# The delta rule's inverse on four corners of the TensorE array, with the column decay made by TensorE

## The reference, cut to what matters

```
L[i, j] = beta_i * exp(g_i - g_j) * (k_i . k_j)     for j before i, 0 elsewhere
T       = (I + L)^-1
w, u    = T @ (beta * exp(g) * k),  T @ (beta * v)
```

## Time and profile before

| | us |
|---|---|
| median of 3 runs | 2218.81 |
| lowest, highest | 2217.07, 2221.3 |
| the profiled execution, its own time | 2219.51 |
| its span | 2217.7 |
| mean granted TensorE clock | 0.972 |
| TensorE busy, of the span | 2094.4 (94%) |
| VectorE busy | 1413.8 (64%) |
| ScalarE busy | 598.6 (27%) |
| GpSimd busy | 1160.8 (52%) |

### The profile page before, as it was taken

How to read it: one execution, slowest core, us unless ns; L and a number is a source line. 1 busy time by engine, 2 the same in 40 slices (tenths; PEclk the granted TensorE clock), 3 DMA queues, 4 the chain that set the end, 5 groups by cost and what they waited for, 6 DMA issues and landing times.

```text
span 2217.7 us, 33444 instructions
## 1 busy us (share of the span) xinstructions
PE 2094.4 (94%) x13922; PEld 1732.4 (78%) x13922; DVE 1413.8 (64%) x1808; ACT 598.6 (27%) x1239; POOL 1160.8 (52%) x664
## 2 busy tenths in 40 slices
PE   6989999999999999999999989989889888999998
PEld 4877788888777767787887668878888767888886
DVE  6366778478665546779578697878666655611622
ACT  2153220122235452220121232356424222200200
POOL 4633667666655444766665333633300555656654
PEclk9999999999999999999999999999999899999999
DMA  5321334334422112334435421112100112323321
GB/s 181 95 68 57 95 114 166 112 100 158 146 75 67 58 30 76 110 105 152 134 95 185 145 95 58 57 42 93 39 4 4 59 49 74 97 94 100 101 86 67
DMA packets 55767, 201.94 MB, mean 91 GB/s; under 512 B 6560, under 2 KB 6816, under 8 KB 54720
## 3 DMA queue, kind: packets, MB, share of 16 engines
q1 hardware_dynamic: 52272, 187.23, 26.1%
q0 software_dynamic: 1840, 9.60, 1.2%
q10 hardware_dynamic: 1504, 2.95, 0.5%
HBM read 194.78 MB, written 4.19 MB: 90 GB/s over the span
## 4 chain that ended last, share of the span: by engine, by line
PE 84%; DVE 9%; ACT 3%; issue 2%; POOL 1%; DMA 0%; SPq 0%; DVEq 0%; POOLq 0%; ACTq 0%
PE bank L536 69%; PE bank L2867 1%; PE bank L3131 1%; PE bank L2863 1%; POOL parts_r L517 1%; PE bank L2852 1%; PE bank L1448 1%; PE bank L1435 1%; PE bank L1940 1%; PE bank L1952 1%; PE bank L1752 1%; PE bank L1425 1%; DVE big L2284 1%; DVE big L2117 0%; POOL parts_r L511 0%
## 5 line engine op out<-in xcount | busy, mean ns | idle before, releaser
L536 PE MATMUL bank<-xn_r,parts_r 128*128 128x512 f32 (+1 forms) x2928 | 916.9, 392 | 37.8 <-DVE mix_r L776 13.5
L536 PE MATMUL bank<-big_r,parts_r 128*128 128x512 f32 x3208 | 925.4, 392 | 2.3 <-POOL parts_r L517 2.3
L517 POOL TENSOR_TENSOR parts_r<-ring,parts_r 128x1024 fp32r<-128x1024 f32 x293 | 738.6, 2521 | 24.4
L511 POOL TENSOR_SCALAR parts_r<-ring 128x1024 fp32r<-128x1024 f32 x293 | 343.9, 1174 | 724.0 <-PE bank L536 711.4
L536 PEld LDWEIGHTS bank<-big_r,parts_r 128*128 128x128 f32 x3208 | 601.9, 189 | 133.8 <-issue 5.1
L536 PEld LDWEIGHTS bank<-xn_r,parts_r 128*128 128x128 f32 x2928 | 554.0, 191 | 163.6 <-issue 39.0
L903 ACT ACTIVATE big<-bank,small 128x512 f32<-128x512 f32 x88 | 68.4, 780 | 409.1 <-DVE big L947 252.0
L932 DVE TENSOR_TENSOR bank<-bank,nb 128x512 f32<-128x512 f32 x88 | 61.3, 699 | 140.6 <-PE bank L536 140.6
L3398 DVE SCALAR_TENSOR_TENSOR h<-bank,vecs,h 128x512 f32<-128x512 f32 x24 | 17.9, 750 | 173.2 <-PE bank L536 173.2
L3472 DVE TENSOR_TENSOR big<-big 128x512 f32<-128x512 f32 x32 | 82.7, 2586 | 71.0 <-ACT big_r L3453 71.0
L547 DVE TENSOR_TENSOR big_r<-big,big_r 128x512 fp32r<-128x512 f32 x76 | 105.7, 1393 | 0.4
(11 more groups left out here) (460 smaller groups left out, 2767.6 us busy)
## 6 DMA issues: line engine op xcount, KB each, us to landing
ring<-weights SPq DMA_DIRECT2D x295, 512.0 KB, 3.6
cst<-mod_w SPq DMA_DIRECT2D x48, 512.0 KB, 3.9
h<-x SPq DMA_DIRECT2D x8, 256.0 KB, 7.7
h_store<-h POOLq DMA_DIRECT2D x8, 256.0 KB, 2.3
big<-consts POOLq DMA_DIRECT2D x2, 1024.0 KB, 8.9
h<-h_store POOLq DMA_DIRECT2D x1, 2048.0 KB, 8.9
out<-mix SPq DMA_DIRECT2D x8, 256.0 KB, 2.2
cst<-consts SPq DMA_DIRECT2D x1, 1300.0 KB, 11.8
```

What stands on the lines that cost most here:

```text
L511: pool.tensor_scalar(rounded(unit_parts(u)[0]), ring[:, u % RING], 1.0, 0.0, ALU.mult, ALU.add)\
L517: pool.tensor_tensor(rounded(lo), ring[:, u % RING], value(hi), ALU.subtract).then_inc(part_ready, 1)
L536: mm = pe.matmul(ps, rounded(w[a]), rounded(x[b]), start=(start and n == 0), stop=(stop and n == 2))
```

## The change

The inverse's matrix `X` of a cell now lies in the other half of the partitions than its `TT`.

- `gram` and `decay_rows` write to the other half (`across`), so `L`, `A` and `X` lie there. `product_x` takes both operands from that half and writes to the cell's own: the corners (64, 0) and (0, 64) in turn.
- Level 0 sets `X = I - A`. `turn_T` makes two things of it in one loop: its transpose (bank `3 + j`, which ScalarE copies to `Tm`, in the other half) and a copy moved to the cell's own half (bank `j`, which VectorE copies to `TT`). `STEPS` counts one step of TT more than `LEVELS`.
- `product_y` issues y and yt of one cell behind each other. y goes from the cell's own half to the other, yt from own to own; with the two halves in turn this uses all four corners.
- The column's -g_j is added by TensorE: `decay_rows` gets 16 more products, each of a 64x64 slice of g with a selector of -1, accumulated onto the same bank. They are also made for the four decays of `attend`. `decay_act` becomes one exponential over 512 columns in place of eight over 64.
- On VectorE the three loops over the units (L, then A, then TT with the mask of level 1) become one loop of four operations for each unit, followed by a loop that copies TT out of the bank; in the second group that copy waits for `right_u`. On TensorE and ScalarE the turn of a unit comes in its own round, and not one round later.

The level masks, the subtractions, the right sides and `attend` are otherwise as before.

```
-        sell[AG["decay"] + r, r] = sell[AG["beta"] + r, r] = 1
+        sell[AG["decay"] + r, r, 0:CH] = sell[AG["beta"] + r, r, 0:CH] = 1
+        sell[AG["decay"] + r, r, CH:] = -1
...
+        across = rows2[::-1]
+        cells = [(cols(bb, hd), r, x) for bb in range(2) for hd in range(GH) for r, x in zip(rows2, across)]
...
-        def decay_rows(pe, b_, d, pair, sel_, done, reader):
+        def decay_rows(pe, b_, d, pair, sel_, done, reader, place):
             for hd in range(GH):
-                for c, r in enumerate(rows2):
-                    mm = pe.matmul(ps[r, hd::GH], sel_[64:P, GH * d + hd, 0:CH], g_[:, 2 * pair[0] + c:2 * pair[1] + c + 1:2],
-                                   start=True, stop=True)
+                for c, r in enumerate(place):
+                    pe.matmul(ps[r, hd::GH], sel_[64:P, GH * d + hd, 0:CH], g_[:, 2 * pair[0] + c:2 * pair[1] + c + 1:2],
+                              start=True, stop=False)
+                for bb, b in enumerate(pair):
+                    for c, r in enumerate(place):
+                        mm = pe.matmul(ps[r, GH * bb + hd], g_[:, 2 * b + c], selL[64:P, GH * d + hd, CH:2 * CH],
+                                       start=False, stop=(bb == 1))
...
             def turn_T(u):
-                ps = grab(pe, SETS + j, dl(f"c{j}"), LEVELS * q + 1)
-                for c, r in cells:
-                    mm = pe.matmul(ps[r, c], TT[r, c], eye_c[r, :], start=True, stop=True)
+                turned = grab(pe, SETS + j, dl(f"c{j}"), LEVELS * q + 1)
+                moved = grab(pe, j, dl(f"TT{j}"), STEPS * q + 2)
+                for c, r, x in cells:
+                    pe.matmul(turned[x, c], X[x, c], eye_c[x, :], start=True, stop=True)
+                    mm = pe.matmul(moved[r, c], eye_c[x, :], X[x, c], start=True, stop=True)
...
             def product_x(u, n):
-                    mm = pe.matmul(ps[r, c], A[r, c], Tm[r, c], start=True, stop=True)
+                    mm = pe.matmul(ps[r, c], A[x, c], Tm[x, c], start=True, stop=True)
...
             def product_y(u, n):
-                    for c, r in cells:
-                        mm = pe.matmul(ps[r, c], TT[r, c], X[r, c], start=True, stop=True)
-                    mm.then_inc(dl(f"y{j}"), 1)
-                ps = grab(pe, j, dl(f"TT{j}"), LEVELS * q + n + 1)
-                for c, r in cells:
-                    mm = pe.matmul(ps[r, c], X[r, c], TT[r, c], start=True, stop=True)
+                yt = grab(pe, j, dl(f"TT{j}"), STEPS * q + n + 2)
+                for i, (c, r, x) in enumerate(cells):
+                    if n < LEVELS - 1:
+                        mm = pe.matmul(y[x, c], TT[r, c], X[r, c], start=True, stop=True)
+                        if i == len(cells) - 1:
+                            mm.then_inc(dl(f"y{j}"), 1)
+                    mm = pe.matmul(yt[r, c], X[r, c], TT[r, c], start=True, stop=True)
...
         def decay_act(act, ready, i, dst, done):
-            for bb, b in enumerate(pair):
-                for hd in range(GH):
-                    ins = act.activation(dst[:, cols(bb, hd)], dst[:, cols(bb, hd)], ACT.Exp,
-                                         bias=gd_sc[:, 0, b, GH * d + hd:GH * d + hd + 1])
+            act.activation(dst, dst, ACT.Exp).then_inc(dl(done), 1)
...
         def inverse_dve(dve):
                         dve.tensor_tensor(L, bank[j][:, :], X, ALU.mult).then_inc(dl("LT"), 1)
-                    for u in three:
                         dve.wait_ge(dl("LT"), u + 1)
                         dve.tensor_tensor(v8(A), v8(L), wide(level(d, 0)), ALU.mult).then_inc(dl(f"A{j}"), 1)
+                        dve.wait_ge(dl(f"A{j}"), LEVELS * q + 1)
+                        dve.tensor_tensor(v8(X), wide(eye_c), v8(A), ALU.subtract).then_inc(dl(f"TT{j}"), 1)
+                        mask_level(u, 1)
                 for u in three:
-                        dve.wait_ge(dl(f"A{j}"), LEVELS * q + 1)
                         if q:
                             dve.wait_ge(dl("ups"), 2 * (u - SETS) + 2)
-                        dve.tensor_tensor(v8(TT), wide(eye_c), v8(A), ALU.subtract).then_inc(dl(f"TT{j}"), 1)
-                        mask_level(u, 1)
+                        dve.tensor_copy(work[j][4], bank[j][:, :]).then_inc(dl(f"TT{j}"), 1)
```

More of the change, by code:

```diff
@@ L2823, in gram @@
                     for hd in range(GH):
-                        for r in rows2:
+                        for r, x in zip(rows2, across):
                             k_ = gd_k[0:GDN_D, hd, tokens(b, r)]
-                            mm = pe.matmul(ps[r, cols(bb, hd)], k_, k_, start=True, stop=True)
+                            mm = pe.matmul(ps[x, cols(bb, hd)], k_, k_, start=True, stop=True)
                 mm.then_inc(dl("gram"), 1)
@@ L2909, in attend @@
                     mm.then_inc(dl("qk"), 1)
-                decay_rows(pe, 7, d, pair, selA, "at_g", (dl("at_E"), i + 1))
+                decay_rows(pe, 7, d, pair, selA, "at_g", (dl("at_E"), i + 1), rows2)
             for q in range(GROUPS + 1):
@@ L2921, in inverse_pe @@
                         right_w(u - SETS)
-                    if q < GROUPS and u % SETS:
-                        turn_T(u - 1)
+                    if q < GROUPS:
+                        turn_T(u)
                     if q:
                         right_u(u - SETS)
-                if q < GROUPS:
-                    turn_T(SETS * q + SETS - 1)
                 if q == GROUPS:
@@ L2936, in inverse_pe, with decay_act @@
                         attend(n - 1)
-        def decay_act(act, ready, i, d, pair, dst, done):
+        def decay_act(act, ready, i, dst, done):
             act.wait_ge(dl(ready), i + 1)
-            for bb, b in enumerate(pair):
-                for hd in range(GH):
-                    ins = act.activation(dst[:, cols(bb, hd)], dst[:, cols(bb, hd)], ACT.Exp,
-                                         bias=gd_sc[:, 0, b, GH * d + hd:GH * d + hd + 1])
-            ins.then_inc(dl(done), 1)
+            act.activation(dst, dst, ACT.Exp).then_inc(dl(done), 1)
         def inverse_act(act):
@@ L2973, in inverse_act @@
                     for u in three:
-                        d, pair, j, _ = unit_of(u)
-                        decay_act(act, "E", u, d, pair, work[j][2], "D")
+                        decay_act(act, "E", u, work[u % SETS][2], "D")
                 for u in three:
@@ L2978, in inverse_act @@
                         take_w(u - SETS)
-                    if q < GROUPS and u % SETS:
-                        copy(u - 1, 0)
+                    if q < GROUPS:
+                        copy(u, 0)
                     if 0 < q < GROUPS:
                         take_u(u - SETS)
-                if q < GROUPS:
-                    copy(SETS * q + SETS - 1, 0)
                 if q == GROUPS:
@@ L2990, in inverse_act @@
                     if q == 0 and n <= TB:
-                        p, d = divmod(n - 1, 2)
-                        decay_act(act, "at_E", n - 1, d, (CB + 2 * p, CB + 2 * p + 1), at_decay[d], "at_D")
+                        decay_act(act, "at_E", n - 1, at_decay[(n - 1) % 2], "at_D")
         def inverse_dve(dve):
@@ L3080, in inverse_dve @@
                     if q < GROUPS:
-                        d, pair, j, _ = unit_of(u)
-                        L, A, X, Tm, TT = work[j]
-                        dve.wait_ge(dl(f"A{j}"), LEVELS * q + 1)
+                        j = u % SETS
+                        dve.wait_ge(dl(f"x{j}"), LEVELS * q + 1)
                         if q:
                             dve.wait_ge(dl("ups"), 2 * (u - SETS) + 2)
-                        dve.tensor_tensor(v8(TT), wide(eye_c), v8(A), ALU.subtract).then_inc(dl(f"TT{j}"), 1)
-                        mask_level(u, 1)
+                        dve.tensor_copy(work[j][4], bank[j][:, :]).then_inc(dl(f"TT{j}"), 1)
                 if q == GROUPS:
```

19 lines of the change are left out of this document (8 added, 11 removed).

## The result

The changed kernel takes 2227.49 us (median of 20 runs, 2218.13 to 2233.03) against 2221.11 for the kernel before (20 runs on the same chip, 2214.31 to 2228.78). The ratio is 1.0026, 95% interval [1.0016, 1.0036]: slower by about a quarter of a per cent, where 2204 was predicted.

What follows compares the result with a forecast made beforehand. TensorE sets 84% of the span; in the inverse's stage TensorE, VectorE or ScalarE bounds by part. +4.9 - 12.8 - 0.3 - 7.8 (group two's levels) + 1.5 = -14.5 us: 2205.0 profiled, 2204 median, range 2198 to 2222.

Steps and rivals of the forecast that it cites:

- The rate of a corner: `product_y` on four corners: a record each 14.6 ns, a unit's 64 records in 0.93 us where it took 1.87.
- rival B: Four corners give less: 23 ns a record whatever its columns, TensorE's level 7.2 us, 2213 us in all; chance 15%.
- C: y and yt of a cell leave two corners at work; `product_y` keeps 1.87 us, +8, 2227 us; chance 12%.
- D: A cell's second product can't start its weights before the first is done: 2.8 us a unit, 2249 us; chance 3%.
- First prologue: Start of the inverse's stage to group one's level 1: decays partly at half clock, then VectorE's path, +4.9 us on 16.35.
- Group one: First three units' five levels: 54.7 us become 41.9, -12.8 us.
- the halved `product_y`: Group one, four levels: 11.2 us of the gain.
- four decays: Group one: `attend`'s decay products on TensorE take back 3.7 us.
- ScalarE's block: Group one: the 2.02 us block of exponentials gone from between the levels, 5.3 us of the gain.
- Second prologue: Before group two's levels, 23.1 us: longer decays, last turn no longer waits, level 1 at +22.8, -0.3 us.
- The new copy: VectorE's copy of a whole bank of TT: between 0.47 and 0.69 us, taken as 0.61.
- Clock: Low granted clock stretches stay and one may be added through TensorE's gaps: +1.5 us, between 0 and 4.

Runs made afterwards that it cites:

- the pairs: Changed kernel, level products made for two cells at a time, half as many products, part of the result wrong: 2205.48 us against 2219.91 before.
- ScalarE's new order: Kernel before, attention's `decay_act` moved behind the next level's copies: 2216.06 us, ratio 0.9966; the same on four corners with exponentials back on ScalarE: 2212.35 us, 0.9958.
- the decay alone: Kernel before with only the column decay moved to TensorE, in wide products, one exponential a decay, two corners: 2226.40 us, ratio 1.0026.
- four corners without the decay: Changed kernel with the column decay back on ScalarE as eight exponentials, constant bias, result wrong: 2217.27 us, ratio 0.9983.
- idle corners filled: Kernel before with an added 64x64-weight, 4-column product on an idle corner for each `product_x` product in group two: 2235.72 us against 2222.41 before.
- the alternating weights: Kernel before with an added 32-weight-column, 4-streamed-column product ahead of each `product_x` product in group two: 2346.14 us.

## Why the prediction was wrong, step by step

**The rate of a corner: right, and not enough.** 14.6 ns a record is what the timeline shows inside `product_y`, between the stops. The step that failed is the next one, that a unit's 64 records then take 0.93 us and "TensorE's level falls from 8.40 to 5.6 us, so VectorE becomes the bound". The evidence for the rate were two bursts of 16 records, 32 instructions each with their weight loads; both fit many times into a block of 256. The argument against rival B, that the columns set the pace, was about the array, and nothing in the prediction asked what feeds it. A level is 288 records, 576 instructions: 576/256 x 3.6 to 4.0 is 8.1 to 9.0 us; the kernel before had 8.4. So group two stayed (41.4 in place of 31.9), and the pairs, which need half as many, gave 31.4.

By the 25 ns floor of the Trainium skill ("TensorE: Matmul & The Clock Gate", Part 1) y and yt could not start 14.6 ns apart; the timeline says they do, for a stretch. The row-group rule of the Trainium skill (the same page, Part 3, What overlaps and what doesn't), by which a weight load waits for a running product in the same rows, falls too: y and yt of a cell share their rows, and a record still starts each 14.6 ns in the mean, where one lasts 220 ns. Over a whole level the mean is 29 ns, for another reason than either.

**Rivals.** B gave 2213, with 23 ns for a record of any width; the 14.6 ns of the timeline refute it, and group two lost its whole gain, not 2.8 us of it. C came near in the time (group two nothing, first prologue +6.8, 2227), but its mechanism, that y and yt leave only two corners at work, is refuted by the timeline and by the 31.4 us of the pairs, and its other terms missed (group one -2.5 against +2.2, second prologue +2.5 against -0.2). The time that C gave is right for a wrong reason. D did not occur.

**First prologue: right, with the clock's help.** +5.7 against +4.9, and VectorE's steps to the tenth: last `masked` at +9.8, right sides to +12.6, X of unit 3 at +20.3. A decay at full clock (in the second prologue a head starts each 0.45 us, 1667.35, 1667.80 and so on) is the forecast 1.80; the 0.8 us too little is the clock, which stayed at 0.50 instead of coming back after 6.8 us. That decays 2 and 3 ran at half speed at all was taken from one trace, and was luck: with the clock full there, the same instructions lasted 18.6 us, 2.3 more than in before's trace.

**Group one: -12.8 forecast, +2.2 measured.** Of the 11.2 for the halved `product_y` little is left: in ScalarE's new order group one takes 47.3 us on four corners and 47.8 on two. Part of it is the supply (TensorE waits 5.7 us for issue in the changed kernel's group one), part the clock, and the runs don't separate the two there. The 3.7 for four decays was right by its rate. ScalarE's block was taken at 5.3; made shorter it is worth about 4.1 (the decay alone), and moved away it is worth 7, before's 6.8 us of low clock gone with it. The clock's part: the stretches of 6.8 and 10.2 us hold 124 and 145 records, which at 29 ns would need 3.6 and 4.2 us; so about 9 us were lost there, by an estimate from these rows; before has two stretches of 3.4 us with 71 and 60 records, by the same working 3 us lost, and 1.5 more were forecast. Before's block between the levels was a loss with a cheaper cure than the change's: a place in a list.

**Second prologue: right.** Level 1 at +22.8, as forecast. The new copy takes 0.69 us alone, where 0.61 back to back was taken; it costs nothing there.

**Clock: wrong in size.** +1.5 us, between 0 and 4, was forecast; 24 us more at half speed lie in the stage. In the profiled executions it is 23.9 us of low clock without the decay products in place of 41.0; the decay alone has 30.7 against before's 17.1; ScalarE's order, with its waits gone, 10.2; and the changed kernel with pairs, decay products and all, 20.5. One execution each doesn't settle it. Over all runs the mean granted clock of the whole program is 0.970 for the decay alone, as for before beside it, 0.969 for four corners without the decay, as for before beside it, and 0.967 for the changed kernel. So the decay alone costs its 5.4 us without a lower mean clock, and the mean clock is lower only with both together. Why it stays low over 12.6 us of a busy TensorE is open. Open is also the path on which the instructions come: that 256 of them take at least some 3.4 us while the queue's packets themselves take 1.2 is measured, what fills the rest isn't.

## What to carry to other kernels

Before a stream of small products is made faster in the array, count its instructions: here a weight load and its product could not be sustained under some 28 ns (52.0 us for 1838 of them with idle corners filled), so only wider products (fewer instructions for the same columns) turn four corners into time. A rate read from a burst holds for a burst; look for one as long as the stream that it is to price. And when an engine waits in order for something late, first move the wait behind the work queued after it: four calls moved were worth more than the whole change.

## What was not expected of the hardware

TensorE's instructions come in blocks of 256 (16 KB), 3.4 to 4.2 us apart in the stretches of group two where it waits for them; where fewer are needed they come less often (5 in 31.4 us with pairs). Changing between 64x64 and 64x32 weights from product to product costs some 0.3 us a pair at full clock (0.41 against 4 x 0.029), and a pair took 0.59 us at the clock of 0.50. The granted clock stayed at 0.50 for 12.6 us in which TensorE was busy all the time with products of 64 rows, and with the alternating weights for 30.5 us, busy in all of them.
